# Two-unit first tiles and residuals ahead of the modulation's sums, in a two-block transformer kernel

## The reference, cut to what matters

```python
for layer in range(DEPTH):                       # DEPTH = 2
    m_lat = jnp.split((cond_lat @ mod_w[layer] + mod_b[layer])[:, None, :], 6, axis=-1)
    m_ctx = jnp.split((cond_ctx @ mod_w[layer] + mod_b[layer])[None, None, :], 6, axis=-1)
    h_lat = modulate(rms_norm(x, norm_g[layer, 0]), m_lat[0], m_lat[1])
    h_ctx = modulate(rms_norm(ctx, norm_g[layer, 0]), m_ctx[0], m_ctx[1])
    ...                                          # y_ctx, y_lat from the mixer
    x = x + m_lat[2] * y_lat
    x = x + m_lat[5] * swiglu(modulate(rms_norm(x, norm_g[layer, 1]), m_lat[3], m_lat[4]),
                              ffn_w_in[layer], ffn_w_out[layer])
    ...                                          # the same for ctx in layer 0
```

## The kernel before, in words

| layer | modulation tiles before | sums |
|---|---|---|
| eo (4 tiles) | 16, both conditions | 32 |
| f0o, half 0 (8 tiles) | 24, both conditions; each t starts with the gate that its own residual needs | 48 |
| f0o, half 1 (8 tiles) | 32, latent alone | 32 |
| rg (8 tiles, layer 1's mixer gate) | none | 0 |

## Time and profile before

### The profile page before, as it was taken

One profiled execution on the slowest core, in us unless ns is written; L12 is line 12 of the kernel. 1 busy time (PEld: TensorE's weight loads), 2 busy tenths in 40 slices (PEclk: granted clock), 3 DMA queues, 4 the chain that ended last, 5 costly groups with the idle time before them and its releaser, 6 DMA issues. The chain is left out here.

```text
span 3330.2 us, 38997 instructions
## 1 busy us (share of the span) xinstructions
PE 2964.7 (89%) x15588; PEld 2404.5 (72%) x15588; DVE 1252.2 (38%) x1869; ACT 1007.1 (30%) x1476; POOL 992.6 (30%) x482
## 2 busy tenths in 40 slices
PE   2789888578998999789998998999989999999998
PEld 1677787467887888668944776788758777887686
DVE  6456554563147116223013215611063554303523
ACT  2235544213311221331203223222243334324432
POOL 0130232112222222344301332444334433342343
PEclk7899999688999999889999998999999999999999
DMA  5200110231134116432210223432211110021121
GB/s 192 104 28 1 39 44 14 97 118 51 59 120 156 63 43 232 138 110 97 77 38 25 76 101 142 170 105 93 84 52 51 34 44 32 33 96 62 48 92 63
DMA packets 48957, 268.50 MB, mean 81 GB/s; under 512 B 5552, under 2 KB 6832, under 8 KB 28592
## 3 DMA queue, kind: packets, MB, share of 16 engines
q1 hardware_dynamic: 48816, 266.54, 22.9%
HBM read 264.42 MB, written 2.10 MB: 80 GB/s over the span
## 5 line engine op out<-in xcount | busy, mean ns | idle before, releaser
L413 POOL TENSOR_TENSOR shared_w_lo<-stage,shared_w_hi 128x2048 fp32r<-128x2048 f32 (+1 forms) x127 | 549.5, 4327 | 1392.0 <-ACT shared_w_hi L386 1392.0
L529 POOL TENSOR_TENSOR shared_w_lo<-stage,shared_w_hi 128x512 fp32r<-128x512 f32 (+2 forms) x233 | 301.2, 1323 | 516.1 <-ACT shared_w_hi L521 514.4
L386 ACT CAST shared_w_hi<-stage 128x2048 fp32r<-128x2048 f32 (+1 forms) x127 | 224.5, 1768 | 509.4 <-PEq L367 135.5
L453 PE MATMUL f0i_acc<-norm_b_hi,shared_w_hi 128*128 128x512 f32 x704 | 186.2, 346 | 26.1 <-DVE norm_b_lo L697 13.2
L453 PE MATMUL f0i_acc<-norm_b_lo,shared_w_hi 128*128 128x512 f32 x704 | 184.7, 344 | 0.0
L453 PE MATMUL f1i_acc<-norm_e_hi,shared_w_hi 128*128 128x512 f32 x352 | 140.1, 398 | 9.5 <-DVE norm_e_lo L697 8.0
L453 PEld LDWEIGHTS f0i_acc<-norm_b_hi,shared_w_hi 128*128 128x128 f32 x704 | 110.1, 193 | 45.1 <-issue 23.3
L596 PE MATMUL two_acc<-norm_f_hi,shared_w_hi 128*128 128x512 f32 (+1 forms) x312 | 131.7, 422 | 9.1 <-DVE norm_f_lo L697 9.1
L521 ACT CAST shared_w_hi<-stage 128x1024 fp32r<-128x1024 f32 (+2 forms) x117 | 114.6, 1023 | 82.6 <-PE last_acc L596 43.9
L453 PE MATMUL f1i_acc<-norm_e_lo,shared_w_hi 128*128 128x512 f32 x352 | 138.9, 394 | 0.0
L789 DVE TENSOR_TENSOR ffn_hidden<-f0i_acc,ffn_gate 128x512 f32<-128x512 f32 (+1 forms) x44 | 22.5, 552 | 307.4 <-PE f0i_acc L453 307.4
(11 more groups left out here) (544 smaller groups left out, 6983.0 us busy)
## 6 DMA issues: line engine op xcount, KB each, us to landing
stage<-in_w_f0i SPq DMA_DIRECT2D x22, 1024.0 KB, 4.9
stage<-in_w_f1i SPq DMA_DIRECT2D x22, 1024.0 KB, 4.8
mod_slots_d<-in_w_mod SPq DMA_DIRECT2D x32, 512.0 KB, 4.0
stage<-in_w_rv SPq DMA_DIRECT2D x16, 1024.0 KB, 4.9
mod_slots_a<-in_w_mod SPq DMA_DIRECT2D x24, 512.0 KB, 4.9
mod_slots_c<-in_w_mod SPq DMA_DIRECT2D x24, 512.0 KB, 3.5
stage<-in_w_rqk SPq DMA_DIRECT2D x12, 1024.0 KB, 4.9
mod_slots_e<-in_w_mod SPq DMA_DIRECT2D x24, 512.0 KB, 5.5
```

The lines of the kernel that those rows point to most:

```text
L386: nc.scalar.copy(w_hi[:, slot, 0:size], stage[:, slot, 0:size]).then_inc(hi_ready, 1)
L413: nc.gpsimd.tensor_tensor(w_lo[:, slot, 0:size], stage[:, slot, 0:size], w_hi[:, slot, 0:size].bitcast(F32), ALU.subtract)\
L453: mm = nc.tensor.matmul(out[0:min(P, nt), b, 0:m], w[:, k, unit[1]:unit[1] + min(P, nt)], x[:, k, s:s + m], start=begin, stop=end)
L529: last = nc.gpsimd.tensor_tensor(w_lo[:, index % 2, part], stage[:, index % 2, part], w_hi[:, index % 2, part].bitcast(F32), ALU.subtract)
```

## The change

Part one: in a first tile whose source gives chunks, with two units, TensorE takes each chunk of x into both units before it waits for the next (`by_chunk`); the `w_lo` products of both units follow. It applies to aq, eo, f0i half 0, ckv0, rqk and f1i half 0.

Part two: `beside` takes the place of `spread` in four layers. Of the modulation tiles of a weight tile t, those that its own residual needs are summed ahead of it, and the others behind it. The tiles are shared out anew: f0o half 0 has 18 (8 gates and 10 of layer 1), half 1 has 14 (6 for both conditions, 8 for the latents), rg has the last 24 (latents), six weight tiles with 4 each. eo keeps 16, as 6, 5, 5, 0. The conditions for f0o are loaded once, behind the norm of f0i half 0 and into the norm's work buffers, and used by both halves.

```diff
@@ linear: the first tile
+def by_chunk(hi, lo, units):
+    pe.wait_ge(hi_ready, ring.split + 1)
+    for k in range(kc):
+        pe.wait_ge(made["ready"], made["first"] + k + 1)
+        for u, unit in enumerate(units):
+            if k == 0:
+                wait(pe, unit_free, c0 + u - 1)
+            for xi, x in enumerate((x_hi, x_lo)):
+                for b, (s, m) in enumerate(unit[2]):
+                    nc.tensor.matmul(acc[0:P, (c0 + u) % 2, b, 0:m], hi[:, k, unit[1]:unit[1] + P],
+                                     x[:, k, s:s + m], start=k == 0 and xi == 0, stop=False)
+    pe.wait_ge(lo_ready, ring.tile + 1)
+    for u, unit in enumerate(units):
+        for k in range(kc):
+            ...                                  # lo[:, k] with x_hi, as before
+        mm.then_inc(unit_done, 1)
@@ linear: VectorE's work of a tile
     side["dve"](dve, t)
     evac_dve(dve, t, j, counts(t), results(j))
+    side["dve_after"](dve, t)
@@ modulation: beside(needed, free, then, conds_at)
+def of_sp(sp, t):
+    if t == 0 and not again and conds_at is None:
+        load_conds(sp)
+    for n in range(ahead[2 * t], ahead[2 * t + 2]):
+        load(sp, n)
+def of_dve(dve, t):
+    for n in range(ahead[2 * t], ahead[2 * t + 1]):
+        sum_up(dve, n)
+    if needed[t]:
+        dve.wait_ge(mod_summed, sums_before(ahead[2 * t + 1]))
+def behind(dve, t):
+    for n in range(ahead[2 * t + 1], ahead[2 * t + 2]):
+        sum_up(dve, n)
+    ...                                          # behind the last: wait, then the scales
@@ the four users
-    return made["spread"](0, len(tiles), DC, scale_mixer_1)       # f0o half 0, 24 tiles
+    free = [2, 2, 2, 1, 1, 1, 1, 0]                                # 18 tiles
+    return conds_c[0]["beside"]([1] * DC, free, conds_at="loaded")
-    return made["spread"](0, 32, DC, scale_ffn_1)                 # f0o half 1, 32 tiles
+    return made["beside"]([0] * DC, [2] * 7 + [0], scale_mixer_1)  # 14 tiles
+    return made["beside"]([0] * 8, [4] * 6 + [0, 0], scale_ffn_1)  # rg, 24 tiles
-    return made["spread"](0, 16, 4, scale_ffn)                    # eo
+    return made["beside"]([0] * 4, [6, 5, 5, 0], scale_ffn)
@@ f0i half 0, at the end of SyncE's queue
+def conds_behind_norm(sp):
+    sp.wait_ge(norm_sem["lo"], norm_done["lo"])
+    sp.dma_start(conds_c[0]["at"], io["conds"][:, 0:2, :]).then_inc(conds_landed, 16)
```

More of the change, by code:

```diff
@@ L337, in linear @@
         def linear(name, x_hi, x_lo, units, evac_act=None, evac_dve=None, source=None, ahead=False,
-                   loads=(), side=None):
+                   loads=(), side=None, behind=None):
             n, kc, nt = shapes[name]
@@ L377, in _ @@
                                 side["sp"](sp, t)
+                        if behind is not None:
+                            behind(sp)
                     @block.scalar
@@ L428, in _ @@
                             made["pe"](pe)
+                        def by_chunk(hi, lo, units):
[12 more added lines that the diff above has]
+                                for k in range(kc):
+                                    for b, (s, m) in enumerate(unit[2]):
+                                        mm = nc.tensor.matmul(acc[0:P, (c0 + u) % 2, b, 0:m], lo[:, k, unit[1]:unit[1] + P],
+                                                              x_hi[:, k, s:s + m], start=False, stop=k == kc - 1)
+                                mm.then_inc(unit_done, 1)
                         def body(t, j, last):
@@ L432, in body @@
                             lo = w_lo[:, slot_of(j), 0:words].rearrange("p (k n) -> p k n", k=kc)
+                            if made and made["ready"] and isinstance(t, int) and t == 0 and U == 2:
+                                by_chunk(hi, lo, units_of(0))
+                                return
                             for u, unit in enumerate(units_of(t)):
@@ L472, in body @@
                                 evac_dve(dve, t, j, counts(t), results(j))
+                            if side is not None and "dve_after" in side:
+                                side["dve_after"](dve, t)
                         if evac_dve or side is not None:
@@ L645, in source @@
                     squares, rstd, total = home
+                    if total is None:
+                        total = psum(scope, f"norm{n}_total", [P, 2, 512])
                 else:
@@ L755, in program, with feed_forward @@
         ffn_done = [1]
-        def feed_forward(layer, x_hi, x_lo, segs, residual, source, in_side=None, out_side=()):
+        def feed_forward(layer, x_hi, x_lo, segs, residual, source, in_side=None, out_side=(), behind=None):
             T = sum(m for _, m in segs)
@@ L798, in feed_forward @@
                         linear(f"f{layer}i{half}", x_hi, x_lo, feature_units(segs), evac_act, evac_dve,
-                               source if half == 0 else None, ahead=True, side=in_side(inner) if in_side and half == 0 else None)
+                               source if half == 0 else None, ahead=True, side=in_side(inner) if in_side and half == 0 else None,
+                               behind=behind if half == 0 else None)
                     with ExitStack() as inner:
@@ L850, in program, with modulation @@
         mod_begun = dict(slots=[0] * MOD_SLOTS, sums=0, conds=0)
-        def modulation(tiles, conds, buffer, product):
+        def modulation(tiles, conds, buffer, product, again=False):
             slots = buffer.shape[1]
@@ L857, in modulation @@
             mod_begun["sums"] += sum(len(whos) for _, _, whos in tiles)
-            mod_begun["conds"] += 1
+            if again:
+                conds_base -= 1
+            else:
+                mod_begun["conds"] += 1
             for n in range(len(tiles)):
@@ L917, in spread, with beside, of_act @@
                 return dict(sp=of_sp, act=of_act, dve=of_dve)
-            return dict(load_conds=load_conds, silu_conds=silu_conds, load=load, sum_up=sum_up, spread=spread,
+            def beside(needed, free, then=None, conds_at=None):
+                ahead = [0]
+                for t in range(len(needed)):
+                    ahead += [ahead[-1] + needed[t], ahead[-1] + needed[t] + free[t]]
+                assert ahead[-1] == len(tiles)
+                def of_sp(sp, t):
[3 more added lines that the diff above has]
+                        load(sp, n)
+                def of_act(act, t):
+                    if t == 0 and not again:
+                        silu_conds(act)
+                def of_dve(dve, t):
[6 more added lines that the diff above has]
+                        sum_up(dve, n)
+                    if free[t] and ahead[2 * t + 2] == len(tiles):
+                        dve.wait_ge(mod_summed, sums_before(len(tiles)))
+                        if then is not None:
+                            then(dve)
+                return dict(sp=of_sp, act=of_act, dve=of_dve, dve_after=behind)
+            return dict(load_conds=load_conds, silu_conds=silu_conds, load=load, sum_up=sum_up, spread=spread, beside=beside,
                         sums_before=sums_before)
@@ L2132, in program, with gate_linear @@
         gates_done = [0]
-        def gate_linear(name, x_hi, x_lo, buf, func, other=None, ahead=False, source=None):
+        def gate_linear(name, x_hi, x_lo, buf, func, other=None, ahead=False, source=None, side=None):
             n = shapes[name][0]
@@ L2159, in evac_dve @@
                             nc.vector.tensor_tensor(o, o, b, ALU.add).then_inc(unit_free, 1)
-                linear(name, x_hi, x_lo, feature_units(ONLY_LAT), evac_act, evac_dve, source, ahead)
+                linear(name, x_hi, x_lo, feature_units(ONLY_LAT), evac_act, evac_dve, source, ahead,
+                       side=side(scope) if side else None)
         weights = ExitStack()
         share_weight_buffers(weights)
-        gate_linear("rg", n1_hi, n1_lo, qk_ret, ACT.Silu, ahead=True, source=ret_norm)
+        gate_linear("rg", n1_hi, n1_lo, qk_ret, ACT.Silu, ahead=True, source=ret_norm, side=rest_of_layer_1)
         normed_1.close()
```

26 lines of the change are left out of this document (19 added, 7 removed).

## The result

The changed kernel takes 3308.3 us (median of 5 runs, 3303.1 to 3314.3); the kernel before takes 3332.6 on the same footing (5 runs, 3328.7 to 3337.9). The ratio is 0.9929, 95% interval 0.9911 to 0.9947: 24 us faster. The forecast was 3306. The profiled execution took 3308.32 with a span of 3306.5, against 3332.02 and 3330.2.

The account below looks back on a forecast made before the run. Reachable losses: slow norm chunks, VectorE's sums ending f0o's halves, and eo's 13.6 us wait. Terms 19.7 + 10.9 + 8.5 + 1.0 - 12.0 = 28.1 us off 3332.0 gave 3303.9; with the median 5.1 higher, forecast 3306, range 3290 to 3324.

Parts of the forecast that it names:

- First tiles: Chunks into both units: gains aq 4.2, f0i half 0 5.8, rqk 4.5, f1i 3.2, ckv0 2, eo 0; sum 19.7 us.
- rival (a): In the chunk phases of first tiles the clock does not hold, losing 11 us in all: 3317; chance 0.17.
- (d): First tiles give nothing, since the next tile's weights come too late: 3326; chance 0.04.
- f0o: Fewer sums behind the last tiles let VectorE end soon after TensorE: half 0 gains 10.9 us, half 1 8.5.
- a PEq wait of about 4 us: Sign at f0i half 1: TensorE's PEq waits there would be about 4 us instead of 12.9.
- eo: VectorE bounds this stage either way; TensorE waits 8.8 us between tiles 1 and 2; gain 1, between -3 and 4.
- 724 to 727: In eo, the time in us at which the ten sums behind tile 2 end; the last residual at 729.4.
- rg: Added loads and sums stall TensorE 10.7 us, plus 1.3 for the clock: 12 lost; a load pair lands in 4.0.
- a clock that falls once: In rg, 1.3 us of the forecast loss, for TensorE's clock falling once.
- f0o half 1's price: 2.6 us a sum with its waits; used for rg as 4 x 2.6 + 1.4 = 11.8 us a tile.
- Rival (b): rg loses 25 us instead of 12, more loads being late behind 1 MB stage loads: 3319; chance 0.11.
- Rival (c): rg's two slots give 17 us a tile; 37 lost plus 14 for clock drops of 2.3 each: 3348; chance 0.05.

Follow-up runs that it names:

- e1: The kernel before with its first tiles taken by chunk and no other edit: 3315.9 us against 3331.9, ratio 0.9954.
- e2: The changed kernel with `by_chunk` never taken, so only the sums' new order and shares: 3327.4 us, ratio 0.9983 to the kernel before.
- e4: The changed kernel with three modulation tiles per weight tile in rg (18) and six more in f0o half 1: 3290.9 us, ratio 0.9873 to the kernel before.
- e10: The changed kernel with its new shares, but all sums of a tile ahead of its residual again: 3332.3 us, ratio 1.0003 to the kernel before.

## Why the prediction was right, and where it was off

**First tiles: right.** Forecast 19.7; measured 4.7 + 2.2 + 1.7 + 4.3 + 1.6 = 14.5. eo, which I had set at 0, gained 1.6 with the old order (e1), but nothing that shows with the new one: 89.1 without `by_chunk` (e2), 88.6 to 91.0 with it. f0i: at its second tile the gain is nearly the forecast one, 27.3 us from the stage's first matmul to that tile before, 22.0 now: 5.35 against 5.8. The other 3.2 went where no term of the sum looked: a unit of f0i half 0 took 8.32 us before and 8.48 after, and half 1 the other way round, which is 3.5 of its unforecast gain of 4.1. In e4's trace a unit of half 0 took 8.32 again, and the stage 191.8 us: 5.6 less than before. Of f1i's 3.2 the trace has 3.1 at the second tile (18.2 to 15.1), and 1.4 are given back at the end: the wait ahead of f1o grew from 4.1 to 5.5, because VectorE is as slow as TensorE there and its sums end the stage. Once it had risen the clock held in the chunk phases, so rival (a) is out, and (d) too.

**f0o: right** by the mechanism named. e10 shows that the smaller shares did it and not the order. That both halves came out within 0.3 us of the forecast is luck in half 0: with this code it took 95.3 to 97.9 us in the other traces, and 107.7 and 110.0 with the old one. The sign that I named for it, a PEq wait of about 4 us, does not fit my own sum, which has VectorE end 1.2 us behind TensorE and the next stage 0.75 later; the wait was 2.0.

**eo: undersized.** 4.0 instead of 1. VectorE does bound the stage, as said, and the 8.8 us wait came to the tenth. The ten sums behind tile 2 met no split, and ended 83.1 us after the stage's first matmul, the lower end of my "724 to 727" (83 to 86); the last residual follows them at once, instead of 2 us or more later. In the other traces with this order and these shares eo takes 89.1 (four traces, one of them without `by_chunk`: 89.1 or 89.2) or 91.0, so 0.5 to 2.4 of the 4.0 are luck of the collisions.

**rg: the step that was mis-sized.** The forecast loss was 12, the measured one 18.7. The stalls behind the first results were 0, 2.9, 1.75, 3.3, 0.3 and 3.5 us, 11.8 in all, where the prediction had 0, 1.3, 3.7, 0.9, 2.3 and 2.4, 10.7. That looks right, with only the clock missed: 1.3 us for "a clock that falls once" against matmuls that were busy 7.4 us longer. And 11.8 + 7.4, less 0.4 of a shorter first wait, is the loss of 18.7. But this sum hides the cause. From the end of one stall to the end of the next pass 14.53, 14.50, 14.31 and 14.66 us, whether the clock fell between them or not. That is VectorE's period, and TensorE has no part in it. Where the clock fell, TensorE was slower and waited less at the next tile (1.75 and 0.28 us); where it did not, it waited longer (3.33 and 3.46). Only behind the last stall does VectorE's chain no longer hide the clock: the last tile's matmuls took 12.8 us instead of 11.0.

By the chain the loss is 17.5 us between tile 2's first matmul and tile 7's, counted from 0 (71.9 us instead of 54.4), 1.7 for the clock behind it, less 0.6 at the start. So what failed is the 10.7 us of stalls, that is VectorE's pace, which cost 17.5, and the agreement with the measured stalls is luck. The 1.3 us for the clock held, at 1.7. Two steps made the pace too fast. The prediction let a pair of loads land in 4.0 us; in rg the load that SyncE issues 1.1 us behind the 1 MB stage load took 5.8 to 6.0 us in every tile, and the others 3.4 to 4.4. And the 12 was backed by f0o half 1's price, which gives 11.8 us a tile: against TensorE's 10.9 that loses 5 us over six tiles and not 12.

Rival (b), more loads late behind stage loads, was thus right about part of the mechanism, and 18.7 lies halfway between the forecast's 12 and its 25. Rival (c) had 2.3 us for each fall of the clock, near to the 7.4 in three, but added them to VectorE's period, where they are hidden; its period of 17 us was not reached.

**The total.** My terms sum to 28.1, and came to 19.3; f0i half 1 gave 4.1 beside them and the rest of the program 0.3. The swing of f0i's two halves cancels (3.2 lost, 3.5 of the 4.1 won), so what the total missed is rg's 6.7 and f1i's 1.6, less eo's 3.0. By that sum the profiled execution should have taken 3303.9, and it took 3308.3. That the forecast median, 3306, lies nearer to the measured one is luck: 2 us had been added to the sum, and eo's gain covers part of rg's loss.

## What to carry to other kernels

Work put behind a result instead of ahead of it is not removed but moved one tile later: do it with shares that leave the last tile empty, or it lands on the end of the stage. When a stage is filled with a second stream of work, price its period (here four sums, one collision, 3.9 us of landings) against the first stream's. Where the second stream sets the pace, its period is the cost: do not add TensorE's slow clock to it, except behind the last stall. Here a quarter less load brought the period under the bound as well as four slots with an operand in PSUM did (103.5 and 103.4 us), because another stage had the idle time to take that quarter.

## What the hardware showed beyond that

A pair of matmuls (512 and 256 columns) takes 0.347 or 0.353 us at granted clock 1.00, the same value through a whole stage, and which of the two changes between executions of code that is identical up to there. TensorE in two windows of f0i, half 0 and half 1 (window, length, busy and matmuls, clock, DMA share, GB/s), first in the changed kernel, then in e4, whose code is the same up to f0o's half 1, behind both windows:

```profile
800.00:900.00 100.00, 100.00 (x568) 1.00 0.17 57
1070.00:1200.00 130.00, 130.00 (x752) 1.00 0.16 55
```

```profile
800.00:900.00 100.00, 100.00 (x579) 1.00 0.18 63
1070.00:1200.00 130.00, 130.00 (x738) 1.00 0.16 57
```

568 against 579 matmuls in the same 100 us, and in the other half the reverse. f0o shows it as 11.66 or 11.44 us a tile. It is worth up to 3.6 us in each half of f0i and 1.8 in each half of f0o, and with the 13 us of the second block, whose cause stays open too, it would account for most of the scatter of one kernel's times (3302 to 3317 for e1). What chooses the value stays open: no run was made for it.
